# Second block of a two-block transformer kernel: per-piece layer-norm statistics, spatial products alternating with gate tiles, own tiles for rotated q and k, gate tiles between the last head's sums

## The reference, cut to what matters

```
h = _rmsnorm(x, g_pre_mix)
proj = h @ w_in
q, k, v, g, u, sv, a_ret, a_sgu = jnp.split(proj, ...)      # 512 512 1024 1024 1024 1024 1024 1024 columns
y_ret = _retention_branch(q, k, v, g, ret_decay_logit, w_ret_o)
y_sgu = _sgu_branch(u, sv, sgu_ln_g, sgu_ln_b, w_spatial, b_spatial, w_sgu_o)
merged = jax.nn.sigmoid(a_ret) * y_ret + jax.nn.sigmoid(a_sgu) * y_sgu
x = x + _rmsnorm(merged @ w_out, g_post_mix)
```

## Time and profile before

| what | us |
|---|---|
| median of three runs | 2410.36 |
| lowest and highest of them | 2404.33, 2412.18 |
| the profiled execution, as timed | 2406.64 |
| span of its trace, first to last instruction | 2404.8 |
| mean granted TensorE clock | 0.974 of full |

### The profile page before, as it was taken

The page is one execution under the profiler, slowest core; times in us unless marked ns, Lnnn a source line. Parts: engine busy times, 40 slices in busy tenths (PEclk is TensorE's granted clock), DMA queues, the critical chain, the costliest instruction groups (busy, mean ns, idle before and its releaser), DMA issues.

```text
span 2404.8 us, 29981 instructions
## 1 busy us (share of the span) xinstructions
PE 2299.0 (96%) x10848; PEld 1895.6 (79%) x10848; DVE 1426.7 (59%) x1802; ACT 987.3 (41%) x1353; POOL 128.9 (5%) x145
## 2 busy tenths in 40 slices
PE   6899999999998899999999999899998996999996
PEld 5688788888886688788888888788887884888885
DVE  7788864444335788865444334743776447888623
ACT  3477544343222487544433223333443423333221
POOL 1000000000001000010000010000000012000010
PEclk9999999999999999999999999989999997999998
DMA  4211222222232211222222233212122221222221
GB/s 144 71 54 55 87 76 100 105 87 94 85 101 87 80 55 54 71 88 101 92 103 78 87 112 116 73 69 111 57 79 75 83 93 38 102 93 99 82 98 65
DMA packets 32641, 204.41 MB, mean 85 GB/s; under 512 B 3616, under 2 KB 4000, under 8 KB 13344
## 3 DMA queue, kind: packets, MB, share of 16 engines
q1 hardware_dynamic: 32544, 203.13, 24.0%
HBM read 201.02 MB, written 2.10 MB: 84 GB/s over the span
## 4 chain that ended last, share of the span: by engine, by line
PE 87%; DVE 7%; issue 3%; ACT 2%; DMA 0%; DVEq 0%; SPq 0%; ACTq 0%
PE mm L1484 27%; PE mm L1486 26%; PE mm L1485 26%; PE misc L1507 1%; DVE conv_y L994 1%; DVE w_lo L924 1%; PE sp L1575 1%; PE ob L1484 1%; PE ob L1485 1%; PE ob L1486 1%; PE sp L1591 1%; PE misc L1616 1%; ACT w_hi L466 1%; PE ob L1584 0%; DVE x L1413 0%
## 5 line engine op out<-in xcount | busy, mean ns | idle before, releaser
L1484 PE MATMUL mm<-in_hi,w_hi 128*128 128x512 f32 x1984 | 793.7, 400 | 50.3 <-DVE w_lo L924 23.1
L1486 PE MATMUL mm<-in_hi,w_lo 128*128 128x512 f32 x1984 | 779.6, 393 | 0.0
L1485 PE MATMUL mm<-in_lo,w_hi 128*128 128x512 f32 x1984 | 779.5, 393 | 0.0
L466 ACT ACTIVATE w_hi<-w_raw 128x2048 fp32r<-128x2048 f32 (+2 forms) x202 | 355.3, 1759 | 692.2 <-PE mm L1486 688.1
L924 DVE TENSOR_TENSOR w_lo<-w_raw,w_hi 128x2048 fp32r<-128x2048 f32 (+2 forms) x205 | 449.6, 2194 | 210.8 <-ACT w_hi L466 210.6
L1484 PEld LDWEIGHTS mm<-in_hi,w_hi 128*128 128x128 f32 x1984 | 377.1, 190 | 144.9 <-issue 37.7
L1485 PEld LDWEIGHTS mm<-in_lo,w_hi 128*128 128x128 f32 x1984 | 377.6, 190 | 80.2 <-issue 4.2
L1486 PEld LDWEIGHTS mm<-in_hi,w_lo 128*128 128x128 f32 x1984 | 376.9, 190 | 80.0
L1484 PE MATMUL mm<-act_hi,w_hi 128*128 128x512 f32 x528 | 205.4, 389 | 0.0
L1485 PE MATMUL mm<-act_lo,w_hi 128*128 128x512 f32 x528 | 205.4, 389 | 0.0
L1486 PE MATMUL mm<-act_hi,w_lo 128*128 128x512 f32 x528 | 205.4, 389 | 0.0
(11 more groups left out here) (352 smaller groups left out, 2814.5 us busy)
## 6 DMA issues: line engine op xcount, KB each, us to landing
w_raw<-in_w_dram SPq DMA_DIRECT2D x149, 1024.0 KB, 4.7
w_raw<-in_w_dram SPq DMA_DIRECT2D x48, 704.0 KB, 3.9
w_raw<-in_w_dram SPq DMA_DIRECT2D x6, 512.0 KB, 5.5
out_dram<-x SPq DMA_DIRECT2D x8, 256.0 KB, 2.0
rope<-in_rope_dram SPq DMA_DIRECT2D x3, 512.0 KB, 3.5
x<-in_x_dram SPq DMA_DIRECT2D x1, 1024.0 KB, 10.5
dist<-in_distances_dram SPq DMA_DIRECT2D x1, 896.0 KB, 5.3
x<-in_x_dram SPq DMA_DIRECT2D x1, 768.0 KB, 7.7
```

Source lines behind the costliest of these rows:

```text
L466: e.activation(whi[:, slot, 0:cols], raw[:, slot, 0:cols], ACT.Copy).then_inc(s_whi, whi_out.up())
L1484: MM(out, ah, bh, start=first, stop=False, **kw)
L1485: MM(out, ah, bl, start=False, stop=False, **kw)
L1486: return MM(out, al, bh, start=False, stop=last, **kw)
```

## The change

Five edits, all in the second block, with the numbers computed as before.

- **Start.** The second `token_major` tile of `sv` moves ahead of the input norm's sums.
- **Statistics.** `bn_stats` runs on each piece of 128 tokens by 256 channels as soon as its gelu is done, 16 pieces within stage 1, instead of 8 pieces of 512 after it; four aggregations are left behind the stage. The high part of `w_sp` is subtracted after them.
- **Spatial products and gates.** All spatial products go to `mm0`; after each comes one gate tile in `mm1`, its sigmoid in `msgu` itself. The weight chunks are laid out as four of `a_sgu`, then four of `w_sgu_o`, and stage 4 is left with 8 output tiles.
- **Heads.** The rounded part of v is read by ScalarE from the bank (with the token scale), and VectorE makes the remainder from the bank in one instruction, which frees the bank; the copy to `sq` is gone. The cosine products are written to own tiles (`q_turned`, `k_turned`) right behind the takes of q and k. ScalarE prepares the chunk before it rounds k. TensorE waits for 4 instead of 8 operand signals.
- **Last head.** The first two tiles of `a_ret` stand one before each of the last two sums, the next two behind them; VectorE and ScalarE follow that order.

```diff
@@ scalar: spatial and gates
-            with L.loop(0, S_SGU // 2) as i:
-                tiles.skip(2)
-                prep(0)
-                e.wait_ge(s_mmf, taken.next(2))
-                e.activation(tA[:, 0:T], tA[:, 0:T], ACT.Sigmoid).then_inc(s_fn, fn.up())
...
+                if ct % 2:
+                    prep(ct // 2 % 2)
+                e.wait_ge(s_mmf, taken.next())
+                e.activation(msgu[:, ct, :], msgu[:, ct, :], ACT.Sigmoid).then_inc(s_fn, fn.up())
...
             def v_hi(b):
-                tiles.skip(1)
-                e.wait_ge(s_mmf, taken.next())
-                hi(rvh[:, b, :], sq[:, b // 2, DV * (b % 2):DV * (b % 2) + DV])
+                e.wait_ge(s_mm, tiles.next())
+                hi(rvh[:, b, :], mm[b % 2][:, 0:DV], rt[:, b:b + 1])
+                taken.skip(1)
...
+                v_hi(0)
+                misc_taken.skip(1)
+                e.wait_ge(s_val, val.next())
+                hi(rqh[:], rqs[:])
+                v_hi(1)
                 prep(h)
+                misc_taken.skip(1)
+                e.wait_ge(s_val, val.next())
+                hi(rkh[:], rks[:])
...
+            tiles.skip(2)
             head_squares()
+            prep(0)
             output_root()
+            for m in range(2):
+                e.wait_ge(s_og, ogs.next())
+                hi(ogh[:, m, :], og[:, m, :])
+            for m in range(2):
+                e.wait_ge(s_mmf, taken.next())
+                e.activation(ar[:, m, :], ar[:, m, :], ACT.Sigmoid).then_inc(s_fn, fn.up())
@@ vector: statistics
+                    def piece(b):
+                        e.wait_ge(s_gel, gel.next())
+                        e.bn_stats(st[:, b, bass.ds(i * 2 + c, 1), :].rearrange("p a b -> p (a b)"),
+                                   sv[:, b, bass.ds(i * 512 + c * 256, 256)]).then_inc(s_do, own.up())
...
+                        if b:
+                            piece(b - 1)
                     prep(c)
+                    piece(TB - 1)
...
-            e.wait_ge(s_gel, gel.next(4 * S_SV))
-            for c in range(TB):
-                e.bn_stats(st[:, 0, :], sv[:, c, 0:512]).then_inc(s_do, own.up())
-                step(e.bn_stats(st[:, 1, :], sv[:, c, 512:1024]))
-                step(e.bn_aggr(mv[:, c, :], st[:, :, :].rearrange("p a b -> p (a b)")))
@@ vector: heads
+                e.wait_ge(s_fn, fn.next())
+                STT(rvl[:, b, :], mm[b % 2][:, 0:DV], rt[:, b:b + 1], r32(rvh[:, b, :]),
+                    ALU.mult, ALU.subtract).then_inc(s_mmf, taken.up())
...
                 take(tA[:, 0:T], 0)
+                turn_a(rqs, tA, 1.0)
                 if hd:
                     centre()
                 take(tB[:, 0:T], 1)
+                turn_a(rks, tB, k_scale)
...
                 v_take(0)
-                rotate(tA, 1.0, rqh, rql)
+                turn_b(rqs, tA, 1.0, rqh, rql)
                 v_take(1)
-                rotate(tB, float(DK) ** -0.5, rkh, rkl)
+                turn_b(rks, tB, k_scale, rkh, rkl)
                 prep(h)
@@ vector: last head
+            take(ar[:, 0, :], 0)
             centre()
+            take(ar[:, 1, :], 1)
+            mean_square(DV, sq[:, 0, :])
+            prep(0)
             gate_output(RH - 1)
@@ tensor
             token_major(0, 0, 0, inp)
+            token_major(0, 1, 1)
             token_sums()
...
-                    ins = mm3(mm[ct % 2][:, n * P:(n + 1) * P], svh[:, n, ct * P:(ct + 1) * P],
+                    ins = mm3(mm[0][:, n * P:(n + 1) * P], svh[:, n, ct * P:(ct + 1) * P],
...
+                if ct % 2 == 0:
+                    e.wait_ge(s_w, w_in.next())
+                out_tile(1, ct // 2 % 2, KT * (ct % 2), xh, xl, KT)
+            pair(yh, yl, sub)
...
-                e.wait_ge(s_sub, sub.next(2 * TB))
+                e.wait_ge(s_sub, sub.next(TB))
...
+            e.wait_ge(s_w, w_in.next())
+            out_tile(0, 0, 0, xh, xl, KT)
             small(ones, sq[:, 0, :], rot)
+            out_tile(1, 0, KT, xh, xl, KT)
             small(ones, sq[:, 0, :], rot)
```

142 lines of the change are left out of this document (76 added, 66 removed).

## The result

The changed kernel takes 2376.2 us (median of four runs, 2372.1 to 2378.8); the kernel before 2410.4 beside it (2404.3 to 2412.2). The ratio is 0.9861, 95% interval 0.9838 to 0.9884. The profiled execution took 2372.1 us, its trace covers 2370.2, and the mean granted clock is 0.984.

The account below looks back on a forecast made before the run. TensorE taken as the bound, so only idle or slow-clock time can be won: -0.9 + 7.7 + 12.6 + 6.5 + 6.0 = 31.9 us, giving 2374.7 from the profiled execution or 2378.5 from the median; middle 2376, range 2366 to 2390.

Parts of the forecast that it names:

- start: Stage 1: moving the second token tile exchanges one idle time for another; cost 0.9 us, bounds gain 1.0 to cost 3.5.
- statistics: Before the first u tile: the 4.9 us wait and slow stretch behind it go; gain 7.7 us, lower bound 5.0.
- spatial and gates: Stages 3 and 4: 97.6 us instead of 110.2 if no bank is waited for; gain 12.6 us, lower bound 8.6.
- heads: Heads 2 to 4 lose two waits, 2.0 us each, the first 0.4; gain 6.5 us, lower bound 3.5.
- last head: Last output product to first gate tile: 6.7 us to win, less a bank wait; gain 6.0 us, bounds 3 and 6.7.
- rival (a): Small margins fail in stage 3, heads, start and last head: 12.6 us for all, 2389, half 2382; chance 0.13 (2384 to 2392).
- rival (c): The clock falls in the new stage 3: stages 3 and 4 take 41 us more than before, total 2430; chance 0.03.
- Just enough: Heads, rotation product of k: VectorE's sine product of q comes 0.9 us earlier, against a wait of 0.68 plus 0.16.
- The predicted gap of 0.7 us at the fifth gate tile: Last head: VectorE takes bank 0 until 1876.9, TensorE wants it at 1876.2.
- my line: Last head: the added-up instructions ahead of VectorE's take of bank 0, root done at 1869.3, take until 1876.9.
- the wait for both sigmoids (to 1874.9): Last head, in the line before the bank 0 take: another table load of 1.28 plus 2 x 0.6 us.
- Rival (b): Clock does not fall at the start, no gap at the last head: 1.9 + 0.7 more, 2373; within the forecast's band.

Follow-up runs that it names:

- token_sum_first: `logs_first_root` plus TensorE's four token sums ahead of the channel-wide one, VectorE's rstd mean and sum clearing behind the first two sv takes: 2368.2 us.
- logs_first_root: Changed kernel with VectorE's small logarithm instructions moved into stage 3 and ScalarE's token-scale root ahead of the rstd one: 2369.1 us.
- start_undone: Changed kernel with the second sv token tile back behind the sums: 2375.6 us, stage 1 56.38 us against 57.55.
- stats_undone: Changed kernel with the sv statistics again as eight 512-column pieces behind stage 1, the w_sp subtraction ahead of them: 2383.7 us.
- heads_undone: Changed kernel with all three head edits undone (v copies, cosine products, ScalarE's preparation order): 2385.1 us, a head 47.15 us against 44.92.

## Why the prediction was right, step by step

The forecast was 2376 and the median is 2376.2. That close a hit has luck in it (the windows won 32.7 us where I had 31.9, and the base was a middle of two), but the terms hold one by one:

| term | predicted | by the two traces | by undoing it |
|---|---|---|---|
| start | -0.9 | -1.26 | -1.17 |
| statistics | 7.7 | 7.77 | 7.19 |
| spatial and gates | 12.6 | 11.98 | 11.83 |
| heads | 6.5 | 7.19 | 7.17 |
| last head | 6.0 | 6.99 | 7.78 |
| sum | 31.9 | 32.67 | 32.8 |

**Start.** Right in sign and cause. The third token tile starts 15.06 us after the first product of the stage, where my working had 14.99. The wait is 6.3 us instead of 5, because the sums, for which I allowed up to 3.4 us, took 1.8 at the higher clock; that changes nothing behind it. The slow stretch was 4.83 us for the 4.4 that I took between 0 and the full length. What I read as 2.75 us of "issue" ahead of the sums is told below.

**Statistics.** VectorE's rows, where the earlier trace rows stood:

```profile
1506.65 2.29 DVE L942 TENSOR_TENSOR w_lo<-w_raw,w_hi 128x2048 fp32r<-128x2048 f32 x1 [1.08 <-ACT w_hi L467]
1509.32 0.63 DVE L1284 BATCH_NORM_AGGREGATE mean_var<-bn 128x2 f32<-128x24 f32 x4
1509.98 0.17 DVE L1286 TENSOR_SCALAR mean_var<-mean_var 128x4 f32<-128x4 f32 x1
1513.91 0.68 DVE L948 TENSOR_TENSOR u_gelu<-mm,rstd 128x512 f32<-128x512 f32 x1
```

The four aggregations take 0.63 us (I had 0.8), a piece 0.42 (I had 0.35), and the take ends at 1514.6. TensorE, which began the stage at 1504.44, wants the bank 10.9 us later, at 1515.3: 0.7 to spare, where I had 0.5.

**Spatial and gates.** VectorE's rows of the first pair, where the earlier trace rows stood:

```profile
1552.41 0.68 DVE L1304 TENSOR_TENSOR tA<-mm,sgu_bias 128x512 f32<-128x512 f32 x1
1554.52 0.69 DVE L966 TENSOR_TENSOR y_lo<-tD,y_hi 128x512 fp32r<-128x512 f32 x1 [0.70 <-ACT y_hi L481]
1555.13 0.68 DVE L948 TENSOR_TENSOR msgu<-mm,rstd 128x512 f32<-128x512 f32 x1
```

The bias ends 5.1 us after the stage's start, the take 7.8, as worked out. No bank is waited for, so rival (a) falls here, and with the clock at 1.00 throughout rival (c) too. The term was 0.6 us too large, since the two stages are 98.24 us and not 97.6: from one spatial tile to the next it is 6.84 us (1547.99 to 1554.83) instead of 1.31 + 5.44 = 6.75. The spatial tile itself is not the slower part: it takes 1.29 us, and the gate tile behind it 5.55. The table load stands once in stage 3, and the activation starts 0.07 us behind its end:

```profile
1554.50 1.28 ACT L759 ACT_TABLE_LOAD   x1
1555.85 0.63 ACT L759 ACTIVATE msgu<-msgu 128x512 f32<-128x512 f32 x1
```

**Heads.** 2.23 us each for heads 2 to 4, where I had 2.0, and 0.5 in the first. The size was right, but its parts were not what I said. I gave the gate tile's 1.2 us to ScalarE's preparation and the single instruction for v together; the runs show that, with the cosine products in their new place, either suffices, and that undoing the preparation's order alone costs nothing. The rotation product's share hangs on the copies (0.80), and only 0.15 on the cosine products. "Just enough" was right: with the cosine products back, 0.15 us is missing.

**Last head.** 6.99 us where I had 6.0. The predicted gap of 0.7 us at the fifth gate tile did not come. ScalarE and VectorE there:

```profile
1840.12 0.63 ACT L478 ACTIVATE sq<-sq 128x512 f32<-128x512 f32 x1
1840.66 1.14 ACT L481 ACTIVATE og_hi<-og 128x512 fp32r<-128x512 f32 x2
1841.81 1.28 ACT L830 ACT_TABLE_LOAD   x1
1843.11 1.15 ACT L830 ACTIVATE sig_ar<-sig_ar 128x512 f32<-128x512 f32 x2
```

```profile
1840.79 0.69 DVE L1365 TENSOR_TENSOR tC<-tC,sq 128x512 f32<-128x512 f32 x1 [0.32 <-ACT sq L478]
1843.20 1.29 DVE L966 TENSOR_TENSOR og_lo<-og,og_hi 128x512 fp32r<-128x512 f32 x2
1844.88 0.69 DVE L966 TENSOR_TENSOR og_lo<-og,og_hi 128x512 fp32r<-128x512 f32 x1 [0.40 <-ACT og_hi L481]
1845.49 0.68 DVE L948 TENSOR_TENSOR sig_ar<-mm,rstd 128x512 f32<-128x512 f32 x1
```

Up to the root my line is exact (16.6 us behind the last output product, counted as in the prediction from the start of what follows it: 1852.74 there, 1824.18 here). The failed step is "the wait for both sigmoids (to 1874.9)", which is 22.2 us behind that product; they were done at 20.1. I had put ScalarE's two roundings `og_hi` behind the last head's products on VectorE. But they are the tiles 0 and 1, the first head's, long ready; ScalarE goes straight on, through a table load, to the sigmoids, beside VectorE's four products. So the bank is free at 1846.2, and TensorE wants it at about 1847.7. Rival (b) had named this half (no gap), without its reason.

**The table loads.** The rows just above show 1.28 us for a load and 0.02 until the next activation, and the last head won 6.99 us, not less than I had said. The Trainium skill (ScalarE: Activation LUTs, "What ACT_TABLE_LOAD costs") adds a drain of 1.38 us to each change of table; these rows don't show it. An estimate by that price: the two changes in this line would have freed the bank 2.8 us later, at 1848.9, some 1.2 us behind TensorE's need, and not the 3 us that I had put at it. No such wait came.

## What to carry to other kernels

A wait is worth its own length and, where the clock falls, the slow stretch behind it. That second part depends on the work that follows, so put dense products behind a wait that can't be avoided; it also depends on when the clock falls, and varied by up to 0.8 us behind the same waits. Where narrow products hang on a long chain of the other engines, set one dense tile that needs nothing of that chain between each two. And where several small edits bear on one wait, try them one by one afterwards: taking one of the three in the heads out again costs nothing, while 22 tiny instructions and the order of two roots, on engines that are no bound, cost 6.7 us together.

## What the runs showed of the hardware

**Clock.** TensorE kept 1.00 behind waits of 0.7 us (`token_sum_first`), 1.0 (`in_lo`) and 1.55 us (`logs_first_root`), and stood at 0.50 behind those of 2.4 to 2.75, 3.5, 4.9 and 6.3 us. The clock fell before such a wait had ended: after's idle 6.29 us have a mean of 0.84. Behind the wait, with dense products, 0.50 lasted 4.3 to 5.7 us, and 2.1 and 3.8 behind the last head's two waits; with the sums behind it and then dense products, 9.4; with spatial tiles, over 19 us, though TensorE was recorded as busy in 19.99 of the 20.00 shown.

**GpSimd beside VectorE.** I had overlooked that two engines with no data in common hold each other up. The last addition to `ssum` on GpSimd and VectorE's preparation start within 0.03 us of each other. In after GpSimd is first by 0.02 us:

```profile
1450.35 1.29 POOL L387 TENSOR_TENSOR ssum<-ssum,sq 128x512 f32<-128x512 f32 x1 [12.76 <-ACT sq L484]
1450.37 3.41 DVE L942 TENSOR_TENSOR w_lo<-w_raw,w_hi 128x2048 fp32r<-128x2048 f32 x1
```

and in before GpSimd's record begins 0.03 us ahead of VectorE's, yet VectorE keeps its pace:

```profile
1453.23 3.43 POOL L386 TENSOR_TENSOR ssum<-ssum,sq 128x512 f32<-128x512 f32 x1 [12.76 <-ACT sq L483]
1453.26 2.29 DVE L924 TENSOR_TENSOR w_lo<-w_raw,w_hi 128x2048 fp32r<-128x2048 f32 x1
1455.46 1.23 DVE L1229 TENSOR_SCALAR small<-pars 128x8 f32<-128x8 f32 x1
```

In both the two together are done 3.43 us after the first start, about the 1.29 and 2.29 us that the unhindered one takes in each pair, one behind the other: in after VectorE's is 1.12 us longer than its usual 2.29, in before GpSimd's is 2.14 over 1.29, and VectorE's next instruction, 0.16 us long in after, takes 1.23. The sums on TensorE start in before 0.1 us behind the end of that addition (1456.66 and 1456.76), so the 2.75 us called "issue" in the earlier trace rows were this wait. `start_undone` repeats it: the addition runs from 1454.75 to 1458.18, the sums start at 1458.28, again behind 2.75 us of "issue". Of the 14 traces three have GpSimd at 1.29 us (after, `stats_undone`, `heads_undone`) and the others at 3.43 to 3.46; where the second token tile stands ahead of the sums, these start right behind it in either case, and stage 1 is the same within 0.1 us in the ten traces that also keep the logarithms there. The Trainium skill (SBUF — State Buffer, "Who interferes with whom") describes such a thing: the two share a pair of ports, a VectorE instruction with two SBUF inputs needs it against a GpSimd instruction that reads SBUF, and it goes as an exclusive lock to whichever is issued first. These rows agree in that one of the two runs at its usual length and the other waits for it. They don't show the order of issue: GpSimd's record begins first in both. Which of them will be first here, and whether an addition that went first would start the sums earlier in the unchanged kernel, was not tried.
